# Maxima products of the next step moved up, and the projections of a step in one group

## The reference

```
s = jnp.einsum('bhqd,bhkd->bhqk', qb, kh).astype(jnp.float32) * scale
s = s + cb[..., :, None] - c[..., None, :]
s = jnp.where(key_pos[None, :] <= q_pos[:, None], s, -jnp.inf)
p = jax.nn.softmax(s, axis=-1)
...
gates = jax.nn.sigmoid(gate_logit + gate_b[l])
merged = (g_a * jnp.einsum('bsc,cd->bsd', y_a, w_up_gdn[l])
          + g_b * jnp.einsum('bsc,cd->bsd', y_b, w_up_fox[l]))
x = x + jnp.einsum('bsd,de->bse', merged, w_out[l])
```

## Time and profile before

| | |
|---|---|
| median of 3 timed runs | 956.7 us (954.65 to 957.1) |
| profiled execution | 955.42 us, span 953.6 us |
| PE busy | 928.5 us (97%), 6380 instructions |
| PEld busy | 700.1 us (73%) |
| DVE busy | 611.6 us (64%), 981 instructions |
| ACT busy | 471.4 us (49%), 842 instructions |
| granted TensorE clock | 0.999 |

### The profile page before, as it was taken

How to read it: one execution, slowest core, us unless ns; L and a number is a source line. 1 busy time by engine, 2 the same in 40 slices (tenths; PEclk the granted TensorE clock), 3 DMA queues, 4 the chain that set the end, 5 groups by cost and what they waited for, 6 DMA issues and landing times.

```text
span 953.6 us, 15908 instructions
## 1 busy us (share of the span) xinstructions
PE 928.5 (97%) x6380; PEld 700.1 (73%) x6380; DVE 611.6 (64%) x981; ACT 471.4 (49%) x842; POOL 19.7 (2%) x28
## 2 busy tenths in 40 slices
PE   5999999999999999999999999999999999999997
PEld 4778787888888876767765666666667888888885
DVE  7487668799999934554576776777763534246262
ACT  7555654633866615533647547466454543334131
POOL 1000002020000000000000000000000000000000
PEclk9999999999999999999999999999999999999999
DMA  7111451249224383332553425234024332223162
GB/s 252 42 48 45 103 170 47 68 171 204 90 89 112 117 247 93 99 99 71 141 170 98 119 83 166 89 105 129 34 68 150 100 104 76 67 111 111 41 193 75
DMA packets 115744, 104.87 MB, mean 110 GB/s; under 512 B 34192, under 2 KB 95760, under 8 KB 115288
## 3 DMA queue, kind: packets, MB, share of 16 engines
q1 hardware_dynamic: 104008, 80.27, 30.1%
q10 hardware_dynamic: 10512, 19.40, 5.5%
q0 software_dynamic: 1152, 4.19, 1.5%
HBM read 76.84 MB, written 27.00 MB: 109 GB/s over the span
## 4 chain that ended last, share of the span: by engine, by line
PE 47%; DVE 2%; ACT 1%; issue 1%; DMA 1%; SPq 0%; DVEq 0%; ACTq 0%
PE pj L2137 6%; PE pj L2139 6%; PE pj L2138 6%; PE pc L2268 3%; PE pa L2236 3%; PE pa L2205 2%; PE pj L2148 1%; PE pj L2150 1%; PE pj L2149 1%; PE pb L2294 1%; PE pa L2240 1%; PE pb L2283 1%; PE pc L2403 1%; PE pa L2403 1%; PE pj L2403 1%; PE pc L2402 1%
## 5 line engine op out<-in xcount | busy, mean ns | idle before, releaser
L144 PE MATMUL pj<-h_hi,w_hi 128*128 128x512 f32 x504 | 203.9, 404 | 0.5 <-DVE w_lo L132 0.5
L145 PE MATMUL pj<-h_lo,w_hi 128*128 128x512 f32 x504 | 197.2, 391 | 0.0
L146 PE MATMUL pj<-h_hi,w_lo 128*128 128x512 f32 x504 | 196.8, 390 | 0.0
L144 PEld LDWEIGHTS pj<-h_hi,w_hi 128*128 128x128 f32 x504 | 94.6, 188 | 23.8 <-issue 1.1
L146 PEld LDWEIGHTS pj<-h_hi,w_lo 128*128 128x128 f32 x504 | 94.7, 188 | 20.3
L145 PEld LDWEIGHTS pj<-h_lo,w_hi 128*128 128x128 f32 x504 | 94.8, 188 | 17.9 <-issue 0.2
L2137 PE MATMUL pj<-h_hi,w_hi 128*128 128x512 f32 x248 | 103.1, 416 | 0.3 <-PEq L315 0.3
L2139 PE MATMUL pj<-h_hi,w_lo 128*128 128x512 f32 x248 | 97.1, 391 | 0.0
L2138 PE MATMUL pj<-h_lo,w_hi 128*128 128x512 f32 x248 | 96.9, 391 | 0.0
L2137 PEld LDWEIGHTS pj<-h_hi,w_hi 128*128 128x128 f32 x248 | 46.6, 188 | 23.5 <-issue 14.5
L569 ACT ACTIVATE xc<-pj 128x512 f32<-128x512 f32 x39 | 23.3, 597 | 73.3 <-PE pj L146 72.6
(11 more groups left out here) (364 smaller groups left out, 1861.2 us busy)
## 6 DMA issues: line engine op xcount, KB each, us to landing
w_raw<-in_w_in SPq DMA_DIRECT2D x48, 512.0 KB, 4.5
fox_scratch<-xc ACTq DMA_DIRECT2D x39, 256.0 KB, 2.4
qkv<-in_x SPq DMA_DIRECT2D x8, 512.0 KB, 6.7
fa<-rows_scratch POOLq DMA_DIRECT2D x8, 512.0 KB, 5.0
rv<-fr_scratch SPq DMA_DIRECT2D x16, 256.0 KB, 4.0
ma<-m_scratch SPq DMA_DIRECT2D x8, 512.0 KB, 4.0
rv<-in_w_out SPq DMA_DIRECT2D x8, 512.0 KB, 3.7
w_raw<-in_x SPq DMA_DIRECT2D x8, 512.0 KB, 4.5
```

Source lines behind the costliest of these rows:

```text
L144: nc.tensor.matmul(o, w_hi[:, slot, k], h_hi[:, k, cols], start=(k == 0), stop=False)
L145: nc.tensor.matmul(o, w_hi[:, slot, k], h_lo[:, k, cols], start=False, stop=False)
L146: last = nc.tensor.matmul(o, w_lo[:, slot, k], h_hi[:, k, cols], start=False, stop=(k == KT - 1))
```

## The change

In the score steps v = 0 to 3, `max_scores(p, 6 + 2v)` of the next step moves up behind `max_scores(p, 5 + 2v)` for v = 1 and 2 (so pieces 8 and 10). For v = 0 the next piece, 6, stays at the start of step 1. The four parts of a step, before one part and then three, stand in one group behind the maxima products, and `square_sums` of the pair before stands ahead of piece 7. On VectorE `row_max` 8 and 10 move with their products. `gated` is taken out of `gate_steps` into `gated_steps`: for step s = 0 it runs in step 0 behind `row_max` 4, for step 0 in step 1 behind `row_max` 6, and from v = 1 on at the end of the step, which now is behind `row_max` 8 or 10.

```diff
@@ VectorE
                     for t in ups_split(g):
                         split_up_lo(t + 2)
+
+                def gated_steps(g):
+
                     for u in units_through(g - 1):
                         if u >= 2:
                             gated(u, gate[:, :], mst[:, :])
...
                         gate_steps(g)
+                        gated_steps(g)
                     elif s == 0:
...
                         spread_max(p, 0)
                         gate_steps(g)
                     elif v < 4:
-                        row_max(p, 4 + 2 * v)
+                        if v < 2:
+                            row_max(p, 4 + 2 * v)
+                            gated_steps(g - 1)
                         if v > 1:
                             add_weights(p, v - 1)
                         row_max(p, 5 + 2 * v)
+                        if v in (1, 2):
+                            row_max(p, 6 + 2 * v)
...
                         gate_steps(g)
+                        if v:
+                            gated_steps(g)
                         if v == 3:
                             spread_max(p, 1)
...
                         gate_steps(g)
+                        gated_steps(g)
@@ TensorE
                     for v in range(4):
-                        max_scores(p, 4 + 2 * v)
+                        if v < 2:
+                            max_scores(p, 4 + 2 * v)
                         key_scores(p, v)
                         past_only(p, v)
                         if v == 0:
                             turn_values(p, 1)
                         else:
                             values(p, v - 1)
-                        fill(1)
-                        max_scores(p, 5 + 2 * v)
                         if v == 1 and p:
                             square_sums(p - 1, 1)
-                        fill(3)
+                        max_scores(p, 5 + 2 * v)
+                        if v in (1, 2):
+                            max_scores(p, 6 + 2 * v)
+                        fill(4)
                     turn_max(p, 1)
```

## The result

The changed kernel takes 960.23 us (median of 5 runs, 959.46 to 961.86) against 955.76 us (5 runs). The ratio is 1.0041, with a 95% interval of 1.0028 to 1.0053, so it is slower by 0.3 to 0.5%. In a later series on another occasion the same kernel had a ratio of 1.0063 (1.0050 to 1.0077). The profiled execution took 961.14 us with a span of 959.3 us, 5.7 us over the span before. 1.0 us of that lies ahead of the attention, where nothing was changed: the turned maxima that open pair 0 (L2222, now L2233) come at 489.13 instead of 488.11. Most of it arose in one place near the start, where this profile has a granted clock of 0.72 from 14 to 20 us and the profile before has 1.00: the product at L144 that waits for `w_lo` comes at 66.78 instead of 66.08. The second profile of the changed kernel has 1.00 there and 66.06.

A forecast was written before the change was run, and what follows sets the result against it. TensorE was taken as busy nearly the whole span, so only its gaps and waits count. Pairs of +2.85, -0.15, -0.1 and +2.25 gave +4.9 us, forecast 961.0 us; own spread 959 to 963, wider range 956.5 to 963.8.

The forecast's parts named there:

- P5 behind R4: Step 0: max_scores 5 waits for VectorE's row_max 4; +0.45 us in pairs 0 and 3, +0.1 in pair 2.
- P8 behind the exponentials of key(1): Step 1: max_scores 8 waits for ScalarE's exponentials of that step's score product; 1.8 us pair 0, 0.8 pair 3, 0.45 pair 2.
- P10 behind the exponentials of key(2): Step 2: max_scores 10 waits for ScalarE's exponentials of that step's score product; 1.1 us pair 0, 1.4 pair 3.
- values(3) of pair 2: Values product of step 3: waits for exponentials hanging on unmoved work, so 0.8 of pair 2's 0.9 us gain is lost.
- The gated product behind R4 in pair 1: Step 0, pair 1: gated product runs after row_max 4, and the group's first projection waits for it; +0.25 us.
- Structure: TensorE order and grouping without waits: -0.5 us in pair 0, -0.4 in each other pair, -1.7 in all.
- By pairs: Sums of the terms: +2.85 us pair 0, -0.15 pair 1, -0.1 pair 2, +2.25 pair 3.
- P10 of pair 0: Sign in the timeline after: max_scores 10 of pair 0 carries TensorE idle time released by ScalarE exponentials; 1.1 us computed.
- the group behind P8 of pair 0: Sign in the timeline after: groups of four projections, as behind max_scores 8, take 2.95 us.
- rival A: Only the grouping counts and waits are covered: structure -1.7 and pair 2's 1.03 us wait, -2.7, so 953.4 us; chance 0.13.
- a change of the tiling mode: Skill's rule that changing mode drains TensorE; by it alone the change is a gain, as mode changes less often in steps 2, 3.

The follow-up runs named there:

- experiment 1: Changed kernel with the gated product again ahead of row_max 4 and 6; 961.66 us against 956.71 for the kernel before, ratio 1.0058.
- experiment 5: Changed kernel with the gate exponential ending step 0 moved behind the exponentials of step 1's score product on ScalarE; 961.65 us against 956.63 before.
- experiment 2: Changed kernel with `plus` and the splits behind it again ahead of row_max 8 and 10; 958.42 us, ratio 1.0016 to the kernel before.
- experiment 4: Kernel before with the grouping of four projection parts alone, VectorE's order unchanged; 957.62 us against 956.71, ratio 1.0010.
- experiment 7: Changed kernel, gated product ahead of row_max 4 and 6 except in pair 2, `plus` ahead of 8 and 10, step 0's projections split; ratio 1.0009 to before.
- experiment 8: As experiment 7, with the exponential of z behind the exponentials of step 2's score product on ScalarE; 954.67 us against 956.63 before, ratio 0.9980.
- experiment 9: Changed kernel with `plus` ahead of row_max 8 and 10, gate and z exponentials later, step 0's projections split; 954.60 us against 956.52 before, ratio 0.9978.

## Why the prediction was right

The time was 960.2 for 961.0 said. The series had the kernel before at 955.8, so the difference was 4.5 us (6.1 in the later series) for 4.9 said. The terms came out one by one:

- P5 behind R4: waits of 0.42 in pairs 0 and 3 (P6 was said to be 0.45 late).
- P8 behind the exponentials of key(1): 1.75 for 1.8 in pair 0, 0.70 for 0.8 in pair 3, 0.25 for 0.45 in pair 2. Experiments 1 and 5 take away the two links (gated product, queue of ScalarE) one at a time, and both times the wait goes.
- P10 behind the exponentials of key(2): 1.34 for 1.4 in pair 3. In pair 0 it is 0.98 for 1.1 in the second profile; in the first the slow group took its place.
- values(3) of pair 2: 1.07 us for 0.8. The size was right by luck, since the reason was not: the prediction had these exponentials hang on work that stays where it was. They hang on `plus`, which the change puts behind R10, and the wait is gone in experiment 2 and in every other one with `plus` ahead of R10.
- The gated product behind R4 in pair 1: the first projection starts 0.45 us behind P5 (556.95 - 556.50) where it started 0.25 behind (553.18 - 552.93), so +0.20 for 0.25.
- Structure: taking the waits off the second profile leaves -0.40 in pair 0 (2.76 - 0.43 - 1.75 - 0.98), -0.25 in pair 2 and -0.23 in pair 3, for -0.5, -0.4 and -0.4.
- By pairs, to the turned maxima: +3.2 in the first and +2.8 in the second profile for +2.85, -0.37 and -0.33 for -0.15, +2.16 and +2.19 for +2.25. Pair 2 to values(3): 22.82 before (635.77 - 612.95) and 22.76 after (639.38 - 616.62), for -0.1. Together +4.95 and +4.58 for +4.85.

Of the signs that the prediction named, two did not show in the first profile: P10 of pair 0 waited nowhere, and the group behind P8 of pair 0 took 4.47 us and not 2.95.

What was off: the prediction held the price of a wait to be its length. TensorE's lower clock behind a long wait was not in it and added about 1.5 us (4.47 - 2.95) in one profile of the two. It left the first profile's pair 0 only 0.4 us over the forecast since P10's wait fell away in the same place, which is luck. Also rival A undervalued what the one projection ahead of P9 and P11 covered (experiment 4): the grouping alone, without the move of P8 and P10, gains nothing. What the Trainium skill says of a change of the tiling mode (TensorEngine Tiling (Array Packing), Key Properties), named in the prediction, agrees with the 0.2 us of a group, but decides nothing here.

A repeated series gave 1.0063 and the first 1.0041, with intervals that barely overlap. The mean granted clocks of the timed runs go with this. In the first series the run at 0.999 took 959.46 us, those at 0.997 took 959.88 and 960.23, those at 0.995 took 961.14 and 961.86. In the later one the run at 0.999 took 960.29 us, those at 0.995 took 961.61 and 962.58, those at 0.993 took 962.97 and 963.03. So at 0.999 the changed kernel is 3.7 and 3.8 us over the median of the kernel before, and what lies above that goes with a lower clock, more often so in the later series. That part of the loss was in no term of the prediction. Where in those runs the clock fell isn't shown, since only one run of each series has a profile.

## What to carry to other kernels

A product that shares a buffer with another engine's reads is bound by that engine's whole queue, so before it is moved up, count everything that stands ahead of its releaser, and what that waits for. Where an engine with slack is in order, move the work that can wait (here a gate exponential and that of z) behind the work that the full engine waits for: the exponential of z alone took experiment 7's ratio of 1.0009 to 0.9980, where the grouping alone gave nothing. A wait taken away at one product can turn up at the next one (P8's 1.75 us as 2.05 at P10) unless the chain behind it gets shorter too.

## What the runs showed of the hardware

TensorE's granted clock fell to its lower level (1.2 GHz) for about 3 us behind four of the long waits: 1.75 us (changed kernel, pair 0, and experiment 2, pair 0), 2.28 us (experiment 1, pair 3) and 2.13 us (experiment 5, pair 0). It did not behind 1.75 us (the second profile of the changed kernel), 2.05 us (experiment 1, pair 0) and 2.29 us (experiment 5, pair 3), nor behind the waits of up to 1.34 us in these kernels' steps. The group of four then took 4.4 to 4.5 us instead of 2.95. In experiment 1 the group began at full clock and slowed with its second and third matmul (starts 0.34, 0.33, then 0.42 and 0.43 us apart, where the group of the earlier trace rows has 0.34, 0.24 and 0.23). So a wait of nearly 2 us can cost 1.5 us more than its length, and whether it does changes from run to run.

The clock also fell near the start of the span, where all kernels are the same, in four of the twelve profiles (the first of the changed kernel and experiments 7, 8 and 9: two-microsecond stretches between 14 and 20 us show 0.50 to 0.86). TensorE waits there in every profile, in the first one of the changed kernel 9.2 us, 0.85 and 1.41 us.

In the timed runs the longer times go with the lower mean clock where the waits are long: 960.44 us at 0.997 to 966.07 at 0.992 in experiment 1, 958.75 at 0.998 to 967.15 at 0.991 in experiment 5.
